# One core, a chain of two transformer blocks: the first mixer's compression with its weights as the stationary operand, and the products of its compressed attention in two lots

## The chip, the core and the metric

The kernel is one program on one core of a Trainium2 chip. Its time is device microseconds from the start to the end of an execution. All data is float32 in memory. Large matrix products are made of three products of rounded halves (float32r tiles `whi`, `wlo`, `xt`); the small ones around the change are plain float32.

## The reference

One block with a hybrid mixer (256 tokens, width 1024) is followed by a second block of two layers. Cut to the part that the change touches, in the first block's mixer:

```python
n_cmp = (S - NSA_CMP_LEN) // NSA_CMP_STRIDE + 1        # 15 blocks of 32 tokens, 16 apart
def compress(raw, pos, w1, w2):                        # raw: 2 groups of 256 tokens x 64
    blocks = raw[:, :, idx] + pos
    return jax.nn.silu(blocks.reshape(B, G, n_cmp, NSA_CMP_LEN * dh) @ w1) @ w2
k_cmp = compress(kc_raw, pos_k, w1_k, w2_k)            # w1: 2048 x 256, w2: 256 x 64
v_cmp = compress(vc_raw, pos_v, w1_v, w2_v)
...
lg = einsum(qc, k_cmp) * scale + tab_g[:, :, rel_bucket(d_cmp)]
p_cmp = masked_softmax(lg, d_cmp >= 0)                 # 8 heads x 256 tokens x 15 blocks
o_cmp = einsum(p_cmp, v_cmp)
return gc[..., 0:1] * o_cmp + gc[..., 1:2] * o_slc + gc[..., 2:3] * o_win
```

## The kernel before

Weights come in units of 128 x 2048 floats (1 MB), loaded by SyncE's queue into three buffers `raw`. For most units ScalarE makes the rounded half `whi` (four buffers, `hi_to`) and VectorE the rest `wlo` (three buffers, `lo_to`); `hi_to(k, act, u)` and `lo_to(k, dve, u)` make all units up to `u` that are not yet made. The four units 6 to 9 of the first mixer (`U_MIX + 6` to `+ 9`) hold the compression's weights `w1` (two for the keys, `s` = 0, two for the values, `s` = 1) and are read straight from `raw`. A buffer of `raw` is free for the next load when its unit has been split, or for these four when TensorE has used it.

Each engine has its own program, written out by hand; semaphores order them. The first mixer on TensorE (`mixer_tensor`) is a loop of 26 steps `i`. In each step `att.tensor` does the ordinary attention of 24 head slots in a pipeline: the scores of slot `i` (2 products), the turn of slot `i - 1` (3 transposes) and the sums of slot `i - 2` (3 products). Behind it `mixer_between_tensor` fills the step with other work, by `i`:

- steps 2 to 5: `compress_tensor(s, half)`, 8 of the 16 row pairs of a block each. `BK` (128 rows x 30 columns: 2 groups x 15 blocks) is the stationary operand, the weights of a row pair (128 x 256) the moving one, and the result, 30 x 256, gathers in bank 4 (`s` = 0) or 5 (`s` = 1).
- step 7: `compressed_tensor` turns the result, by now in `HT` behind a copy by VectorE (`compress_vector`, steps 3 and 5) and Silu by ScalarE (`compress_scalar`, step 6), into 256 x 30 by four transposes (line 1024); `compressed_vector` copies it to `HD`.
- step 8: `cmp_tensor` step 0, the products by `w2`, which wait for `HD`.
- step 12: logits of the compressed attention; steps 14 and 15: its probabilities turned into `CT` (15 rows x 2048).
- step 16: `cmp_tensor` step 5, all 16 products of `CT` with the values `VC`: 15 rows x 128 columns stationary, 15 x 64 moving, into banks 7 and 6. VectorE adds them to the output, gated, in step 16 (`cmp_vector` step 5: four operations, lines 1131 and 1134, through `add_gated`).
- steps 6 to 9, 10 to 13, 14 to 18: projections by units 10 to 15 (three products of rounded halves a piece), 12 or 24 records a step at 256 columns.

On VectorE each step holds the row maxima of slot `i` (lines 837 and 843) and, in two steps of three, the copy of slot `i - 1`'s turned probabilities (line 850), then the other work, `lo_to` of one unit in every second step from 11 to 17 among it. The sums of the third set of heads gather in banks 6 and 7 from step 18 on and so wait until the compressed attention's second half has been added (`sums_need`). Nearly all matmuls are issued by one helper, line 231, and all whole transposes by another, line 242.

A plain float32 product shows in the trace as two records (two passes); a transpose and a product of rounded halves as one.

Of the kernel before, what the change touches and what calls it, by code (L numbers as in the profile page):

```python
# [883 lines left out]
def mixer_tiles(k):  # L884
# [33 lines left out]
    k.HT = ar(k, 2560, 512, "p (s n) -> p s n", s=2)  # L918
# [78 lines left out]
def compress_tensor(k, pe, s, half):  # L997
    b, u = 4 + s, U_MIX + 6 + 2 * s + half
    w = k.raw[u % NRAW]
    pe.wait_ge(*k.s_raw[u % NRAW].after(u))  # L1000
    pe.wait_ge(*k.s_dv.after("bk", 2 * s + 1))
    for l in range(8):
        lp = half * 8 + l
        last = mm(pe, k.P[b][0:30, 0:256], k.BK[:, s, lp, :, :].rearrange("p g n -> p (g n)"),
                  w[:, l * 256:(l + 1) * 256], lp == 0, lp == 15)
    last.then_inc(*k.s_used.inc(u))


def compress_vector(k, dve, s):
    dve.wait_ge(*k.s_used.after(U_MIX + 7 + 2 * s))  # L1010
    dve.e.tensor_copy(k.HT[0:30, s, :], k.P[4 + s][0:30, 0:256]).then_inc(*k.s_ev.inc("ht", s))


def compress_scalar(k, act):
    for s in range(2):
        act.wait_ge(*k.s_ev.after("ht", s))
        act.e.activation(k.HT[0:30, s, :], k.HT[0:30, s, :], ACT.Silu).then_inc(*k.s_ea.inc("ht", s))


def compressed_tensor(k, pe, s):  # L1020
    b = 4 + s
    pe.wait_ge(*k.s_ea.after("ht", s))
    for m in range(2):
        last = pe.e.transpose(k.P[b][:, 30 * m:30 * m + 30], k.HT[0:30, s, 128 * m:128 * m + 128],
                              k.cs[0:30, C_ID:C_ID + 30])
    last.then_inc(*k.s_pe.inc("ht", s))


def compressed_vector(k, dve, s):
    dve.wait_ge(*k.s_pe.after("ht", s))  # L1030
    dve.e.tensor_copy(k.HD[:, s, :, :], k.P[4 + s][:, 0:60].rearrange("p (m n) -> p m n", m=2)).then_inc(*k.s_ev.inc("hd", s))

def cmp_tensor(k, pe, step):
    P = k.P
    if step == 0:
        for s in range(2):
            pe.wait_ge(*k.s_ev.after("hd", s))  # L1040
        pe.wait_ge(*k.s_w2.after())
        for m in range(2):
            mm(pe, P[4][:, 0:30], k.W2[:, m * 128:(m + 1) * 128], k.HD[:, 0, m, :], m == 0, m == 1)
        for g in range(2):
            for m in range(2):
                last = mm(pe, P[4][0:15, 64 + 64 * g:128 + 64 * g], k.HD[:, 1, m, g * 15:(g + 1) * 15],
                          k.W2[:, 256 + m * 64:256 + (m + 1) * 64], m == 0, m == 1)
        last.then_inc(*k.s_pe.inc("kc"))
# [21 lines left out]
    if step == 5:  # L1070
        pe.wait_ge(*k.s_ea.after("ct", 3))
        for h in range(8):
            for a in range(2):
                i = 2 * h + a
                last = mm(pe, P[7 - a][:, h * 64:(h + 1) * 64], k.CT[0:15, i * 128:(i + 1) * 128], k.VC[0:15, h // 4, :])
        last.then_inc(*k.s_pe.inc("oc"))


def cmp_vector(k, dve, step):
# [29 lines left out]
    if step == 5:  # L1109
        dve.wait_ge(*k.s_pe.after("oc"))  # L1110
# [76 lines left out]
def mixer_between_tensor(k, pe, i):  # L1187

    U = U_MIX
# [7 lines left out]
    elif i < 10:  # L1197
        if i == 7:
            for s in range(2):
                compressed_tensor(k, pe, s)  # L1200
# [11 lines left out]
    elif i < 19:  # L1212
        if i < 16:
            cmp_tensor(k, pe, i - 11)
        if i == 16:
            cmp_tensor(k, pe, 5)
# [121 lines left out]
def mixer_vector(k, dve):  # L1338
# [10 lines left out]
    for i in range(26):  # L1349
# [5 lines left out]
        if i == 3:  # L1355
            compress_vector(k, dve, 0)
        if i == 5:
            lo_to(k, dve, U + 10)
            compress_vector(k, dve, 1)
        if i == 7:  # L1360
            for s in range(2):
                compressed_vector(k, dve, s)
# [6 lines left out]
        if i in (11, 13, 15, 17):  # L1369
            lo_to(k, dve, U + 13 + (i - 11) // 2)  # L1370
# [4 lines left out]
        if i == 16:  # L1375
            cmp_vector(k, dve, 5)
# [1922 lines left out]
```

## Time and profile before

| what | value |
|---|---|
| median of 3 runs | 1649.23 us (1644.78 to 1649.86) |
| the profiled execution's own time | 1647.63 us |
| its span, first to last instruction | 1646.3 us |
| TensorE matmul busy | 1616.3 us (98%) |
| VectorE, ScalarE busy | 945.6 us (57%), 786.4 us (48%) |
| mean granted TensorE clock | 0.996 |
| the chain that ended last | TensorE 96%, VectorE 2%, ScalarE 1% |

The span and the 1.3 us around it make the execution's own time. The first mixer's steps 1 to 21 lie between 240 and 348 us of the span. A record's start in the views of time is exact to some 10 ns; its length includes the way through the array, so records in a row overlap, and the pace is read from one start to the next.

### The profile page before, as it was taken

The numbers are of one execution on the slowest core, as the hardware profiler recorded it, in microseconds if no ns is written. First come the engines' busy times: TensorE is split into PE (matmuls) and PEld (weight loads), VectorE is DVE, ScalarE is ACT, GpSimd is POOL, SyncE is SP. The second block draws the span as 40 slices with busy tenths as digits, with TensorE's granted clock in tenths as the row PEclk, the third lists the DMA queues.
The fourth block names the chain that finished last, engine by engine and source line by source line (L and its number), as shares of the span: only waits on it lengthen the run. The fifth ranks groups of instructions, "written<-read, shape, count | busy, mean of one in ns | idle before, by whom it ended". The sixth has DMA issues, their size and how long they took to land.

```text
span 1646.3 us, 29834 instructions
## 1 busy us (share of the span) xinstructions
PE 1616.3 (98%) x13094; PEld 1485.8 (90%) x13094; DVE 945.6 (57%) x1202; ACT 786.4 (48%) x1044; POOL 127.5 (8%) x117
## 2 busy tenths in 40 slices
PE   7999999999999999999998999999999999999998
PEld 7999997889999999999997889999999998899997
DVE  5544464566545655446895684546645474675545
ACT  5444444446444554445754264444544455664443
POOL 0000020000000001000376001000020001001000
PEclk9999999999999999999999999999999999999999
DMA  7744554235554465554420155554655543455551
GB/s 280 282 176 167 178 176 157 99 122 199 180 203 178 157 211 194 184 180 158 178 104 4 54 216 202 194 182 154 238 178 192 186 154 128 154 181 202 183 178 75
DMA packets 40865, 280.67 MB, mean 170 GB/s; under 512 B 4794, under 2 KB 4794, under 8 KB 8864
## 3 DMA queue, kind: packets, MB, share of 16 engines
q1 hardware_dynamic: 39024, 272.40, 46.2%
q0 software_dynamic: 1712, 6.37, 1.1%
q8 instruction: 103, 1.69, 0.4%
q14 instruction: 26, 0.21, 0.0%
HBM read 277.14 MB, written 1.08 MB: 169 GB/s over the span
## 4 chain that ended last, share of the span: by engine, by line
PE 96%; DVE 2%; ACT 1%; issue 1%; DMA 0%; SPq 0%; DVEq 0%; ACTq 0%
PE P L231 93%; PE P L242 2%; ACT whi L205 1%; DMA gb<-gains 0%; PE P L2118 0%; ACT AR L863 0%; DVE AR L371 0%; ACT xt L272 0%; DVE AR L2227 0%; DVE AR L2219 0%; DVE AR L837 0%; DVE wlo L219 0%; DVE sm L1982 0%; DVE AR L331 0%; DVE xt L279 0%
## 5 line engine op out<-in xcount | busy, mean ns | idle before, releaser
L231 PE MATMUL P<-xt,whi 128*128 128x256 f32 x5088 | 934.6, 285 | 3.0 <-ACT whi L205 1.6
L231 PEld LDWEIGHTS P<-xt,whi 128*128 128x128 f32 x5088 | 803.3, 193 | 17.8 <-issue 9.4
L231 PE MATMUL P<-xt,wlo 128*128 128x256 f32 x2544 | 702.9, 283 | 0.0
L219 DVE TENSOR_TENSOR wlo<-raw,whi 128x2048 fp32r<-128x2048 f32 x245 | 559.8, 2290 | 88.1 <-PE P L231 76.5
L205 ACT ACTIVATE whi<-raw 128x2048 fp32r<-128x2048 f32 x245 | 467.5, 1909 | 141.0 <-PE P L231 119.6
L231 PEld LDWEIGHTS P<-xt,wlo 128*128 128x128 f32 x2544 | 489.2, 192 | 0.0
L687 DVE TENSOR_TENSOR AR<-P,AR 128x256 f32<-128x256 f32 x114 | 48.4, 424 | 333.1 <-ACT AR L658 333.1
L658 ACT ACTIVATE AR<-P 128x256 f32<-128x256 f32 x114 | 43.7, 383 | 352.2 <-PE P L231 352.2
L231 PE MATMUL P<-whi,hh 128*128 128x512 f32 x504 | 197.9, 393 | 0.0
L231 PE MATMUL P<-wlo,hh 128*128 128x512 f32 x504 | 196.8, 391 | 0.0
L231 PE MATMUL P<-whi,hl 128*128 128x512 f32 x504 | 196.1, 389 | 0.0
L231 PE MATMUL P<-AR 64*64 64x64 f32 (+8 forms) x2506 | 126.9, 244 | 2.5 <-issue 1.3
L231 PE MATMUL P<-whi,xt 128*128 128x512 f32 (+2 forms) x400 | 123.8, 373 | 0.4 <-DVE xt L2529 0.4
L231 PEld LDWEIGHTS P<-AR 64*64 64x64 f32 (+6 forms) x2506 | 99.1, 144 | 18.2 <-issue 8.7
L231 PEld LDWEIGHTS P<-whi,hl 128*128 128x128 f32 x504 | 94.6, 188 | 20.0
L231 PEld LDWEIGHTS P<-whi,hh 128*128 128x128 f32 x504 | 94.9, 188 | 18.2 <-issue 0.2
L231 PEld LDWEIGHTS P<-wlo,hh 128*128 128x128 f32 x504 | 94.9, 188 | 17.5 <-issue 0.2
L690 DVE TENSOR_TENSOR hl<-AR,hh 128x256 fp32r<-128x256 f32 x126 | 55.6, 441 | 61.0 <-ACT hh L663 61.0
L231 PEld LDWEIGHTS P<-whi,xt 128*128 128x128 f32 x400 | 72.5, 189 | 13.2 <-issue 0.8
L663 ACT ACTIVATE hh<-AR 128x256 fp32r<-128x256 f32 x126 | 52.6, 418 | 63.0 <-DVE AR L687 63.0
L510 POOL TENSOR_SCALAR x<-x 128x1024 f32<-128x1024 f32 x10 | 32.5, 3261 | 577.7 <-DVE AR L687 417.3
L231 PE MATMUL P<-wlo,xt 128*128 128x512 f32 (+2 forms) x200 | 73.1, 365 | 0.0
(226 smaller groups left out, 913.0 us busy)
## 6 DMA issues: line engine op xcount, KB each, us to landing
raw<-ws SPq DMA_DIRECT2D x249, 1024.0 KB, 4.8
gb<-gains SPq DMA_DIRECT2D x14, 512.0 KB, 7.1
AR<-by_distance POOLq DMA_DIRECT2D x1, 3072.0 KB, 19.3
x<-x_in SPq DMA_DIRECT2D x2, 512.0 KB, 4.1
AR<-mem_in POOLq DMA_DIRECT2D x1, 1024.0 KB, 5.4
AR<-gains SPq DMA_DIRECT2D x2, 512.0 KB, 4.7
out<-x SPq DMA_DIRECT2D x2, 512.0 KB, 2.6
cs<-cst SPq DMA_DIRECT2D x1, 737.0 KB, 14.3
```

What stands on the lines that cost most here:

```text
L205: act.e.activation(k.whi[n % NHI][:, :], k.raw[u % NRAW][:, :], ACT.Copy).then_inc(*k.s_hi.inc(u))
L219: dve.e.tensor_tensor(k.wlo[n % NLO][:, :], k.raw[u % NRAW][:, :], k.whi[n % NHI][:, :].bitcast(F32), ALU.subtract).then_inc(*k.s_lo.inc(u))
L231: return pe.e.matmul(o, l, r, start=start, stop=stop, skip_group_check=True)
L242: return pe.e.transpose(o, i, k.cs[:, C_ID:C_ID + 128])
L510: pool.e.tensor_scalar(k.x[:, a, :], k.x[:, a, :], ALPHA / scale, None, ALU.mult).then_inc(*k.s_al.inc(t, a))
L658: act.e.activation(k.SL[:, f % 2, :], gate, ACT.Silu).then_inc(*k.s_sl.inc(t, f))
L663: act.e.activation(hh, k.HF[:, f % 2, :].rearrange("p (a t) -> p a t", a=2), ACT.Copy).then_inc(*k.s_hh.inc(t, f))
L687: dve.e.tensor_tensor(k.HF[:, f % 2, :], up, k.SL[:, f % 2, :], ALU.mult).then_inc(*k.s_hf.inc(t, f))
L690: dve.e.tensor_tensor(hl, k.HF[:, f % 2, :].rearrange("p (a t) -> p a t", a=2), hh.bitcast(F32), ALU.subtract).then_inc(*k.s_hl.inc(t, f))
```

## The change

In `compress_tensor` the operands change places: the weights of a row pair become the stationary operand in two halves of 128 columns (`m`), `BK` (128 x 30) the moving one, and the result is 128 features x 30 blocks for each half, side by side in columns 0 to 59 of the bank. This is the layout of `HD`, so the four transposes, `HT` and VectorE's four copies go, and ScalarE's Silu reads the bank and writes `HD`. The products of the compressed attention are made in two lots of four heads, in steps 16 and 17; their gated addition on VectorE moves from step 16 to 17, and `lo_to` of unit 16 from step 17 to 16.

```diff
 def compress_tensor(k, pe, s, half):
-    b, u = 4 + s, U_MIX + 6 + 2 * s + half
+    u = U_MIX + 6 + 2 * s + half
...
     for l in range(8):
         lp = half * 8 + l
-        last = mm(pe, k.P[b][0:30, 0:256], k.BK[:, s, lp, :, :].rearrange("p g n -> p (g n)"),
-                  w[:, l * 256:(l + 1) * 256], lp == 0, lp == 15)
+        for m in range(2):
+            c = l * 256 + m * 128
+            last = mm(pe, k.P[4 + s][:, 30 * m:30 * m + 30], w[:, c:c + 128],
+                      k.BK[:, s, lp, :, :].rearrange("p g n -> p (g n)"), lp + m == 0, lp == 15)
     last.then_inc(*k.s_used.inc(u))
-def compress_vector(k, dve, s):
-    dve.wait_ge(*k.s_used.after(U_MIX + 7 + 2 * s))
-    dve.e.tensor_copy(k.HT[0:30, s, :], k.P[4 + s][0:30, 0:256]).then_inc(*k.s_ev.inc("ht", s))
 def compress_scalar(k, act):
     for s in range(2):
-        act.wait_ge(*k.s_ev.after("ht", s))
-        act.e.activation(k.HT[0:30, s, :], k.HT[0:30, s, :], ACT.Silu).then_inc(*k.s_ea.inc("ht", s))
-def compressed_tensor(k, pe, s):
-    b = 4 + s
-    pe.wait_ge(*k.s_ea.after("ht", s))
-    for m in range(2):
-        last = pe.e.transpose(k.P[b][:, 30 * m:30 * m + 30], k.HT[0:30, s, 128 * m:128 * m + 128],
-                              k.cs[0:30, C_ID:C_ID + 30])
-    last.then_inc(*k.s_pe.inc("ht", s))
-def compressed_vector(k, dve, s):
-    dve.wait_ge(*k.s_pe.after("ht", s))
-    dve.e.tensor_copy(k.HD[:, s, :, :], k.P[4 + s][:, 0:60].rearrange("p (m n) -> p m n", m=2)).then_inc(*k.s_ev.inc("hd", s))
+        act.wait_ge(*k.s_used.after(U_MIX + 7 + 2 * s))
+        act.e.activation(k.HD[:, s, :, :], k.P[4 + s][:, 0:60].rearrange("p (m n) -> p m n", m=2),
+                         ACT.Silu).then_inc(*k.s_ea.inc("hd", s))
...
-    if step == 5:
+    if step in (5, 6):
         pe.wait_ge(*k.s_ea.after("ct", 3))
-        for h in range(8):
+        for h in range(4 * step - 20, 4 * step - 16):
...
-        last.then_inc(*k.s_pe.inc("oc"))
+        last.then_inc(*k.s_pe.inc("oc", step))
...
-        if i == 16:
-            cmp_tensor(k, pe, 5)
+        if i in (16, 17):
+            cmp_tensor(k, pe, i - 11)
...
-        if i in (11, 13, 15, 17):
-            lo_to(k, dve, U + 13 + (i - 11) // 2)
+        if i in (11, 13, 15):
+            lo_to(k, dve, U + 7 + (i + 1) // 2)
+        if i == 16:
+            lo_to(k, dve, U + 16)
...
-        if i == 16:
-            cmp_vector(k, dve, 5)
+        if i == 17:
+            cmp_vector(k, dve, 6)
```

TensorE in one of the steps 2 to 5, and below the @@ line in step 7 (difference of the two kernels; here one row is one product, shown by its shape out, x is how many stand in a row; `P<-raw,AR` and `P<-AR,raw` are the compression, line 1024 the transposes of `HT`):

```order
 L231 MATMUL P<-AR 128x64 x3
-L231 MATMUL P<-raw,AR 30x256 x8
+L231 MATMUL P<-AR,raw 128x30 x16
 L231 MATMUL P<-AR 128x128
 L231 MATMUL P<-AR 128x256
@@ -1194,5 +1194,4 @@
 L242 MATMUL P<-cs,AR 128x128 x3
 L231 MATMUL P<-AR 128x64 x3
-L1024 MATMUL P<-cs,AR 128x30 x4
 L231 MATMUL P<-xt,whi 128x256 x2
 L231 MATMUL P<-xt,wlo 128x256
```

Each step of the compression has 16 products in the place of 8, and step 7 loses its four transposes.

TensorE in steps 16 and 17, the same view (three of the `128x64` rows in each step are the attention's own sums, the rest the products of `CT` and `VC`):

```order
 L231 MATMUL P<-AR 128x256
 L242 MATMUL P<-cs,AR 128x128 x3
-L231 MATMUL P<-AR 128x64 x19
+L231 MATMUL P<-AR 128x64 x11
 L231 MATMUL P<-xt,whi 128x256 x2
 L231 MATMUL P<-xt,wlo 128x256
@@ -1355,5 +1354,5 @@
 L231 MATMUL P<-AR 128x256
 L242 MATMUL P<-cs,AR 128x128 x3
-L231 MATMUL P<-AR 128x64 x3
+L231 MATMUL P<-AR 128x64 x11
 L231 MATMUL P<-xt,whi 128x256 x2
```

The sixteen products of step 16 stand as eight in step 16 and eight in step 17, behind the sums of each.

VectorE from the maxima of step 16 to the split of unit 16, before (lines 837 and 843 are maxima, 850 a copy for the attention, 1131 and 1134 the gated addition out of banks 7 and 6, 219 the split):

```order
L843 TENSOR_SCALAR sm<-sm 128x2
L1131 TENSOR_TENSOR AR<-P7,sm 128x512
L1134 TENSOR_TENSOR AR<-AR 128x512
L1131 TENSOR_TENSOR AR<-P6,sm 128x512
L1134 TENSOR_TENSOR AR<-AR 128x512
L837 ISA AR,sm<-P2,AR 128x128
L837 ISA sm 128x1
L837 ISA AR,sm<-P2,AR 128x256
L837 ISA sm 128x1
L843 TENSOR_SCALAR sm<-sm 128x2
L850 COPY AR<-P3 128x384
L219 TENSOR_TENSOR wlo0<-raw1,whi1 128x2048
```

And of the change (1113 and 1116 are the lines 1131 and 1134 of before):

```order
L843 TENSOR_SCALAR sm<-sm 128x2
L219 TENSOR_TENSOR wlo0<-raw1,whi1 128x2048
L837 ISA AR,sm<-P2,AR 128x128
L837 ISA sm 128x1
L837 ISA AR,sm<-P2,AR 128x256
L837 ISA sm 128x1
L843 TENSOR_SCALAR sm<-sm 128x2
L850 COPY AR<-P3 128x384
L1113 TENSOR_TENSOR AR<-P7,sm 128x512
L1116 TENSOR_TENSOR AR<-AR 128x512
L1113 TENSOR_TENSOR AR<-P6,sm 128x512
L1116 TENSOR_TENSOR AR<-AR 128x512
```

The split of unit 16 stands ahead of step 17's maxima and copy, the gated addition behind them.

## Rows read from the trace of the kernel before

**Rows 1.** The page: span, TensorE's totals, its granted clock in 40 slices.

```profile
span 1646.3 us, 29834 instructions
...
PE 1616.3 (98%) x13094; PEld 1485.8 (90%) x13094; DVE 945.6 (57%) x1202; ACT 786.4 (48%) x1044; POOL 127.5 (8%) x117
...
PEclk9999999999999999999999999999999999999999
...
```

**Rows 2.** The waits from 240 to 345 us: total, times, longest.

```profile
...
ACT AR L863 <- DVE sm L843: 47.9, 18, 5.9
DVE AR L837 <- PE P L231: 36.5, 16, 4.7
...
```

**Rows 3.** Windows: busy time of each engine, granted clock (PEclk), DMA share.

```profile
...
321.00:324.00 3.00, 3.00 (x28) 2.93 (x27) 0.75 (x5) 1.36 (x5) 0.00 (x0) 1.00 0.60 251
324.00:327.00 3.00, 3.00 (x24) 2.93 (x23) 1.23 (x2) 0.00 (x0) 0.00 (x0) 0.88 0.00 0
...
330.00:333.00 3.00, 3.00 (x16) 3.00 (x15) 2.96 (x5) 2.44 (x5) 0.00 (x0) 0.50 0.00 0
...
```

**Rows 4.** TensorE's matmul groups, shapes apart.

```profile
...
L231 PE MATMUL P<-raw,AR 128*30 128x256 f32 x64 | 14.6, 380 | 0.0
...
L231 PE MATMUL P<-AR 15*128 15x64 f32 x32 | 3.8, 272 | 0.0
...
L231 PE MATMUL P<-AR 128*128 128x30 f32 x4 | 0.6, 267 | 0.0
...
```

**Rows 5.** TensorE in order of time, a compression step.

```profile
...
247.79 3.64 PE L231 MATMUL P<-raw,AR 128*30 128x256 f32 x16
251.36 0.92 PE L231 MATMUL P<-AR 64*128 64x128 f32 x4
...
```

**Rows 6.** TensorE, steps 6 and 7.

```profile
...
267.90 0.92 PE L231 MATMUL P<-AR 64*128 64x128 f32 x4
...
269.73 0.48 PE L231 MATMUL P<-xt,whi 128*128 128x256 f32 x2
...
272.77 0.92 PE L231 MATMUL P<-AR 64*128 64x128 f32 x4
...
275.07 0.51 PE L231 MATMUL P<-xt,whi 128*128 128x256 f32 x2
...
```

**Rows 7.** TensorE inside the products.

```profile
...
322.75 2.50 PE L231 MATMUL P<-AR 15*128 15x64 f32 x21
```

**Rows 8.** TensorE, steps 16 to 18.

```profile
...
319.98 0.92 PE L231 MATMUL P<-AR 64*128 64x128 f32 x4
...
321.21 4.49 PE L231 MATMUL P<-AR 128*128 128x64 f32 x38
325.63 0.51 PE L231 MATMUL P<-xt,whi 128*128 128x256 f32 x2
...
328.00 1.65 PE L231 MATMUL P<-AR 64*128 64x128 f32 x4
...
335.19 0.92 PE L231 MATMUL P<-AR 64*128 64x128 f32 x4
...
340.06 0.92 PE L231 MATMUL P<-AR 64*128 64x128 f32 x4
...
```

**Rows 9.** VectorE, steps 16 and 17.

```profile
...
321.61 0.17 DVE L843 TENSOR_SCALAR sm<-sm 128x2 f32<-128x2 f32 x1
325.74 0.69 DVE L1131 TENSOR_TENSOR AR<-P,sm 128x512 f32<-128x512 f32 x1 [3.96 <-PE P L231]
...
327.91 0.69 DVE L1134 TENSOR_TENSOR AR<-AR 128x512 f32<-128x512 f32 x1
...
330.99 2.28 DVE L219 TENSOR_TENSOR wlo<-raw,whi 128x2048 fp32r<-128x2048 f32 x1
...
```

**Rows 10.** TensorE ahead of the second fall of the clock.

```profile
...
803.27 2.85 PE L231 MATMUL P<-AR 12*128 12x256 f32 x12
...
```

**Rows 11.** Windows, as in rows 3, after that stretch.

```profile
...
807.60:810.90 3.30, 3.30 (x18) 3.30 (x17) 2.64 (x6) 3.30 (x7) 1.53 (x2) 0.50 0.33 134
...
```

More of the change, by code:

```diff
@@ L917, in mixer_tiles @@
     k.CT = ar(k, 13800, 2048)
-    k.HT = ar(k, 2560, 512, "p (s n) -> p s n", s=2)
     k.TM = ar(k, 2560, 512)
@@ L1039, in cmp_tensor @@
         for s in range(2):
-            pe.wait_ge(*k.s_ev.after("hd", s))
+            pe.wait_ge(*k.s_ea.after("hd", s))
         pe.wait_ge(*k.s_w2.after())
@@ L1108, in cmp_vector @@
                             k.GTv[:, :, :, 0], ALU.mult).then_inc(*k.s_dv.inc("cden", 3))
-    if step == 5:
-        dve.wait_ge(*k.s_pe.after("oc"))
+    if step == 6:
+        dve.wait_ge(*k.s_pe.after("oc", 6))
         dve.wait_ge(*k.s_dv.after("cden", 3))
@@ L1197, in mixer_between_tensor @@
     elif i < 10:
-        if i == 7:
-            for s in range(2):
-                compressed_tensor(k, pe, s)
         if i == 8:
@@ L1354, in mixer_vector @@
             dve.e.tensor_scalar(k.QB[:, 2:4, :], to_tiles(k, 5), 0.125, None, ALU.mult).then_inc(*k.s_ev.inc("qb", 1))
-        if i == 3:
-            compress_vector(k, dve, 0)
         if i == 5:
             lo_to(k, dve, U + 10)
[L1359 to L1362, printed above, removed]
         if i == 8:
```

## The prediction

> **What bounds the kernel now.** I read the page first: matmuls fill 1616.3 us of a span of 1646.3 us [rows 1], so a change is worth what it takes off TensorE's own stream, and an engine beside it matters only if TensorE comes to wait for it. The waits of the mixer's steps say who has slack: VectorE waits 36.5 us for TensorE's scores, ScalarE 47.9 us for VectorE's maxima [rows 2]; both are done early in each step and idle for the rest of it. What the other engines save (four copies on VectorE, the shorter way to Silu) is therefore worth nothing by itself. The windows then show the one odd place. The clock column goes from 1.00 to 0.88 and to 0.50 around 324 to 333 us, while TensorE is busy 3.00 of 3 us throughout and the DMA share is 0.00 [rows 3]. It is the lower of the clock's two levels, 1.2 GHz for 2.4, and it comes right behind the products of the compressed attention.
>
> **The compression.** Before, a step has 8 products, 16 records of 256 moving columns; from its first record to the next step's first score 3.57 us pass (251.36 - 247.79) [rows 5]. The change makes 16 products, 32 records, of 128 stationary columns and 30 moving ones. The trace has that shape four times, in 0.6 us together with 267 ns for one: (600 - 267) / 3 = 111 ns from start to start [rows 4]. The products of `CT`, also 128 stationary columns but 64 moving ones, run at (2.50 - 0.27) / 20 = 0.112 us a record [rows 7]. Moving columns between 30 and 64 thus don't matter, the load of 128 stationary columns sets the pace. So a lot takes 32 x 0.112 = 3.58 us, where 3.57 stood: nothing gained, nothing lost. Bounds: at best the change of shape at the entry goes (the array stays at 128 x 128 behind the sums), some 0.1 us a step, -0.4 us in all; at worst the pace is the average with entry and exit, 3.82 / 32 = 0.119 us as worked out below, which is +0.25 a step and +1.0 us in all. I take 0, since the stream is long and the steady pace is the nearest row.
>
> The Trainium skill ("TensorE: Matmul & The Clock Gate", section "LDWEIGHTS (loading the stationary operand)") has a load last its columns over 1.2 GHz, 107 ns for 128 and 25 ns for 30, whatever the rows. The trace agrees within 5 ns; by the page's figure, an estimate, a lot would be 3.42 us and the four lots 0.6 us shorter.
>
> **The transposes.** Step 7, which holds them, has 275.07 - 272.77 = 2.30 us ahead of its projection; step 6 without them 269.73 - 267.90 = 1.83 us [rows 6]. They go: -0.47 us. Silu now waits for the compression's last product (267.9) only and runs in step 6 as before; `HD` is wanted in step 8, from 279.4 on, some 5 us after ScalarE is through it. If that cover were gone, TensorE would stand at step 8 for the remainder.
>
> **The two lots.** Before, steps 16 and 17 take 335.19 - 319.98 = 15.21 us [rows 8]. What they would take at the upper clock follows from undisturbed steps. Attention alone is 1.83 us [rows 6]. Step 18 is 340.06 - 335.19 = 4.87 us [rows 8], so its 24 projection records are 4.87 - 1.83 = 3.04 us, and the 12 of step 16 half of it and the entry, 1.6 us. The 16 products put 325.63 - 319.98 - 1.83 = 3.82 us into step 16 [rows 8]; eight of them put in 3.82 - 16 x 0.112 = 2.03 us. Undivided at the upper clock: 1.83 + 3.82 + 1.6 + 1.83 + 3.04 = 12.12 us, so the fall of the clock costs 15.21 - 12.12 = 3.09 us. Divided: (1.83 + 2.03 + 1.6) + (1.83 + 2.03 + 3.04) = 12.36 us, 0.24 us for the second entry. If the division keeps the clock up: -2.85 us.
>
> Does it? Both falls inside the kernel follow a stretch in which few rows of the array work: here 32 records of 15 rows, 3.7 us with hardly a break; at 803.27 us 12 records of 12 rows over 2.8 us [rows 10], and behind them the clock stands at 0.50 [rows 11]. Lots of 1.8 us, with 1.6 us of full projection and 1.83 us of attention between them, are half as long as the first and two thirds of the second. I take that they keep the clock, without certainty.
>
> **What lies beside.** VectorE in step 17: the last product of a lot ends 325.74 - 319.98 - 1.79 = 3.97 us into the step; the four operations take 327.91 + 0.69 - 325.74 = 2.86 us [rows 9], so banks 6 and 7 are free 6.83 us into it. Step 18 begins at 6.90 us and its sums 1.23 us later (321.21 - 319.98) [rows 8]: 1.3 us of cover. Were it gone, the sums of step 18 would wait, and with them the turn of step 19. The split of unit 16 now starts at 321.61 + 0.17 = 321.78 and takes 2.28 us [rows 9]; it ends at 324.06. Step 17's maxima, queued behind it, need their scores at 325.44 + 0.95 = 326.4 us: 2.3 us of cover. The load that it frees starts 9 us earlier, into windows with a DMA share of 0.00 [rows 3].
>
> **The sum.** 0 - 0.47 - 2.85 = -3.3 us. The profiled execution's own time is 1647.63 us, its span 1646.3 and 1.3 around it; it lies 1.6 us below the median 1649.23. So 1644.3 us for a like execution, 1645.9 us against the median. Its own range is 1643 to 1648, from the bounds above.
>
> **Rivals.** A change within 0.3% (4.9 us) can't be told from none here.
>
> *The clock falls in the compression.* This one ends on the other side. In a lot of 3.58 us each record streams 30 columns in 112 ns, where 256 in some 216 ns streamed before, less than a quarter of the pace (0.27 columns a ns against 1.19). No row shows full-height records with such short streams for microseconds. Against it: the 12-row records move 256 columns each and the clock fell all the same, and the products of `CT` move more columns in the same time than the new compression does; what both stretches share is the few rows, and the compression keeps 128. Also the loads, busy 2.93 of 3 us in such a stream [rows 3], now use all 128 rows. For it: the products' 64 columns are already short, and the fall could be owed to that too. Price: each lot doubles, 3.6 us more, and attention's 1.83 us nearly, so 5 us a step. From the second step on that is three steps, 15 us, and about 3 us until the clock is back behind it, as the fall of now costs; with the gain kept, 18 - 3.3 = +14.7 us, 1664 us. A single short fall is +2 and ends near no change. It decides as soon as two steps run low.
>
> *The clock still falls between the lots.* Attention and a lot together are 3.6 us of thin work, about as long as the lot that brought the fall. Then 0.47 us is gained, 0.24 lost, and up to 3.09 us paid again: 1647 to 1649.5.
>
> *A rule of busy time.* If the clock went by TensorE's idle time alone, nothing in steps 2 to 5 or 16 and 17 would move it, and with TensorE busy 3.00 of 3 us at 0.50 [rows 3] the fall would have a cause outside of these steps: -0.47 + 0.24 = -0.2 us, 1649 us. The Trainium skill ("TensorE: Matmul & The Clock Gate", section "What's actually happening") gates the clock by how busy the engine has been, with the lower level after an idle stretch; read as busy time, the trace does not agree, since no idle time precedes the fall.
>
> *The weight loads are slower than taken.* The 111 and 112 ns are of operands in `AR`, the weights come from `raw`; at the upper bound +1.0, so -2.3 us, 1647 us. It is part of the forecast's range.
>
> **How the numbers follow.** Forecast 0.45; a fall that stays between the lots 0.20; busy time alone 0.05; a fall in the compression 0.30, of which a quarter is one short fall. The first three lie between 1643 and 1650. The range reaches to 1664 for the last and 1642.5 below: 1642.5 to 1664 leaves out what is beyond the price of three steps and a lucky low, under 0.15. Faster by over 0.3% needs 4.9 us, more than the forecast gives, though the fall of now may cost more in other executions than in the profiled one (the runs spread over 5 us): 0.14. Slower: the fall in the compression but for its short form, and a little for a wait not seen, 0.25. Within 0.3%: 0.61.
>
> **What would show it.** Right: the compression's steps still 5.5 us long each with a clock of 1.00 from 245 to 275 us; step 7 without line 1024 and 0.47 us shorter; no 0.50 between 320 and 335; steps 16 and 17 at 5.5 and 6.9 us; VectorE's gated addition over before the sums of step 18. Wrong: 0.50 in the windows from 250 on and compression steps of 10 us; a second lot at 0.22 us a record; TensorE's rows with idle time ahead of the sums of step 18.

## The result: 17 us slower, and the profile after

| | before | after |
|---|---|---|
| median of 4 runs each | 1647.80 us (1644.78 to 1649.86) | 1664.64 us (1661.26 to 1669.19) |
| ratio after / before | | 1.0105, 95% interval 1.0072 to 1.0139 |
| the profiled execution's own time | 1647.63 us | 1669.19 us |
| its span and mean granted TensorE clock | 1646.3 us, 0.996 | 1667.9 us, 0.983 |

The kernel got 16.8 us slower. The profiled execution of the changed kernel is the slowest of its four, 4.6 us above their median, so its account below shows somewhat more than the typical loss. The page of the changed kernel, against [rows 1]:

```profile
span 1667.9 us, 29949 instructions
...
PE 1634.9 (98%) x13154; PEld 1509.8 (91%) x13154; DVE 945.5 (57%) x1198; ACT 785.8 (47%) x1044; POOL 127.8 (8%) x117
...
PEclk9999995999999999999999999999999999999999
...
q8 instruction: 104, 1.70, 0.4%
```

TensorE is as full as before (98%) and busy 18.6 us longer, with 60 records more; VectorE and ScalarE are where they were. No other engine has become the limit. The clock line has a 5 in its seventh slice. Span times (1 - mean clock) gives the time lost to the lower clock: 1667.9 x 0.017 = 28.4 us, where before had 1646.3 x 0.004 = 6.6. The difference, 21.8 us, accounts for the 21.6 us by which the two spans differ (the clocks are rounded to 0.001, which is 1.6 us of a span). The windows of the changed kernel show the place (columns as in [rows 3]):

```profile
246.00:249.00 3.00, 3.00 (x31) 3.00 (x28) 1.06 (x6) 0.99 (x4) 0.00 (x0) 1.00 0.00 0
249.00:252.00 3.00, 3.00 (x23) 2.63 (x22) 0.69 (x5) 0.00 (x0) 0.00 (x0) 0.92 0.22 33
252.00:255.00 3.00, 3.00 (x16) 3.00 (x15) 0.58 (x2) 0.98 (x4) 0.00 (x0) 0.50 0.76 317
...
282.00:285.00 3.00, 3.00 (x15) 3.00 (x15) 1.35 (x6) 2.02 (x5) 0.00 (x0) 0.50 0.91 380
285.00:288.00 3.00, 3.00 (x24) 2.87 (x23) 0.00 (x0) 1.87 (x4) 0.00 (x0) 0.90 0.68 287
...
342.00:345.00 3.00, 3.00 (x17) 2.18 (x15) 1.02 (x6) 0.77 (x2) 0.00 (x0) 0.73 0.73 303
...
348.00:351.00 3.00, 3.00 (x18) 3.00 (x18) 1.76 (x3) 0.00 (x0) 0.00 (x0) 0.59 0.00 0
```

TensorE is busy 3.00 of 3 us in every one of them, and yet its clock stands at 0.50, the lower level of 1.2 GHz for 2.4, from about 251.5 to 285.6 us: the three later lots of the compression and the start of step 6. The last two rows show that it falls around the two lots of the products as well. TensorE's timeline, against [rows 5, 6] (start, length, operation, how many):

```profile
246.68 3.71 PE L231 MATMUL P<-AR,raw 128*128 128x30 f32 x32
250.32 0.92 PE L231 MATMUL P<-AR 64*128 64x128 f32 x4
...
252.78 6.98 PE L231 MATMUL P<-AR,raw 128*128 128x30 f32 x32
259.69 1.65 PE L231 MATMUL P<-AR 64*128 64x128 f32 x4
...
270.04 1.65 PE L231 MATMUL P<-AR 64*128 64x128 f32 x4
...
280.39 1.65 PE L231 MATMUL P<-AR 64*128 64x128 f32 x4
...
287.64 0.92 PE L231 MATMUL P<-AR 64*128 64x128 f32 x4
...
289.47 0.48 PE L231 MATMUL P<-xt,whi 128*128 128x256 f32 x2
...
292.51 0.92 PE L231 MATMUL P<-AR 64*128 64x128 f32 x4
```

The first lot runs at the upper clock: 250.32 - 246.68 = 3.64 us from its first record to the next score, 0.114 us a record. The second takes 259.69 - 252.78 = 6.91 us for the same 32 records. Steps 4 and 5 last 10.35 us each where 5.5 stood. Step 7 has lost its transposes: 289.47 - 287.64 = 1.83 us ahead of its projection for 2.30. Steps 16 to 19, against [rows 8]:

```profile
335.96 0.92 PE L231 MATMUL P<-AR 64*128 64x128 f32 x4
...
337.19 2.70 PE L231 MATMUL P<-AR 128*128 128x64 f32 x22
...
342.38 1.52 PE L231 MATMUL P<-AR 64*128 64x128 f32 x4
...
351.41 0.92 PE L231 MATMUL P<-AR 64*128 64x128 f32 x4
...
352.64 0.78 PE L231 MATMUL P<-AR 128*128 128x64 f32 x6
...
356.28 0.92 PE L231 MATMUL P<-AR 64*128 64x128 f32 x4
```

Step 16 takes 6.42 us and step 17 9.03; together 15.45, where the undivided lot had 15.21. One row of before that is not among those ahead of the prediction, the first score of step 8, closes the account:

```profile
278.14 0.92 PE L231 MATMUL P<-AR 64*128 64x128 f32 x4
```

| stretch of the profiled execution | before | after | difference |
|---|---|---|---|
| up to the first score of step 3 | 251.36 | 250.32 | -1.04 |
| steps 3 to 5 | 16.54 | 30.07 | +13.53 |
| step 6 | 4.87 | 7.25 | +2.38 |
| step 7 | 5.37 | 4.87 | -0.50 |
| steps 8 to 15 | 41.84 | 43.45 | +1.61 |
| steps 16 to 18 | 20.08 | 20.32 | +0.24 |
| all behind | 1306.24 | 1311.62 | +5.38 |
| span | 1646.3 | 1667.9 | +21.6 |

15.4 of the 21.6 us arise in steps 3 to 7. The rows "steps 8 to 15" and "all behind" hold falls of the clock that before's execution doesn't have at these places:

```profile
309.00:315.00 6.00, 6.00 (x51) 5.28 (x51) 3.47 (x7) 0.99 (x4) 0.00 (x0) 0.83 0.19 57
...
897.00:903.00 6.00, 4.67 (x76) 4.11 (x77) 3.17 (x8) 2.49 (x7) 2.54 (x3) 0.75 0.01 3
903.00:909.00 6.00, 4.87 (x115) 4.24 (x113) 3.00 (x7) 1.78 (x6) 3.31 (x4) 0.68 0.01 4
```

The last two windows alone cost 6 x 0.25 + 6 x 0.32 = 3.4 of the 5.38 us. Whether the change brings these two is not shown here; more on it below.

### The profile page after: what moved, and what is told of

Same layout as the page of the kernel before. It is cut to its first block, busy times and chain, and to the rows that moved or that the text cites. A ratio compares the mean times of both kernels' runs of the same rounds, so it can differ in the third digit from the quotient of the medians.

```text
span 1667.9 us, 29949 instructions
## 1 busy us (share of the span) xinstructions
PE 1634.9 (98%) x13154; PEld 1509.8 (91%) x13154; DVE 945.5 (57%) x1198; ACT 785.8 (47%) x1044; POOL 127.8 (8%) x117
## 4 chain that ended last, share of the span: by engine, by line
PE 94%; DVE 2%; ACT 2%; issue 1%; DMA 1%; POOL 0%; SPq 0%; DVEq 0%; ACTq 0%
PE P L231 91%; PE P L242 2%; ACT whi L205 1%; DMA AR<-AR 0%; DMA gb<-gains 0%; DVE wlo L219 0%; PE P L2093 0%; ACT AR L863 0%; ACT xt L272 0%; DVE AR L371 0%; DVE AR L837 0%; DVE AR L2202 0%; DVE xt L279 0%; DVE sm L1957 0%; DVE x L359 0%
## 5 line engine op out<-in xcount | busy, mean ns | idle before, releaser
L231 PEld LDWEIGHTS P<-xt,whi 128*128 128x128 f32 x5088 | 802.5, 193 | 18.6 <-issue 9.4
L231 PE MATMUL P<-AR 64*64 64x64 f32 (+7 forms) x2506 | 132.0, 249 | 3.9 <-issue 2.0
L231 PEld LDWEIGHTS P<-AR 64*64 64x64 f32 (+5 forms) x2506 | 103.3, 148 | 18.5 <-issue 8.9
```

The costliest lines, as they stand in the source:

```text
L231: return pe.e.matmul(o, l, r, start=start, stop=stop, skip_group_check=True)
```

## The experiments

Times are medians, with the lowest and highest run; a ratio is to the kernel before on the same chip in the same session, with its 95% interval. The kernel before had 1648.37, 1648.57 and 1647.74 us in the three sessions (25, 28 and 23 runs). The theory after the result: the clock falls because the new compression streams only 30 columns for each load of 128; the rivals were that the lots or the loads themselves do it. In the diffs, `...` stands for edits that are left out: the ones that carry the same change through to the other engines.

**The two lots alone.** The compression as before, the products of `CT` in steps 16 and 17.

```diff
-    if step == 5:
+    if step in (5, 6):
-        for h in range(8):
+        for h in range(4 * step - 20, 4 * step - 16):
...
-        if i == 16:
-            cmp_tensor(k, pe, 5)
+        if i in (16, 17):
+            cmp_tensor(k, pe, i - 11)
```

> The compression as before (30 columns stationary, 256 moving, transposes in step 7); only the products of the compressed attention in two lots, with the gated addition in step 17 and the split of unit 16 in step 16. Theory S (it is the short streams of the new compression that bring the clock down): no 0.50 between 245 and 290 us, and the time near the kernel before, between -3.1 us (the lots keep the clock) and +1 us (they do not). Rival L (the new order of steps 16 and 17 costs by itself, for instance by a wait of VectorE): several us slower than before, with idle time of TensorE in steps 17 and 18. Rival P (the clock falls by where an execution happens to stand, whatever the compression): a long stretch at 0.50 here too.

Measured: 1647.18 us (1646.37 to 1654.16, 10 runs), ratio 1.0008 (0.9993 to 1.0023). Its timeline of TensorE, first scores of steps 16 to 19:

```profile
321.31 0.92 PE L231 MATMUL P<-AR 64*128 64x128 f32 x4
...
327.75 1.51 PE L231 MATMUL P<-AR 64*128 64x128 f32 x4
...
336.75 0.92 PE L231 MATMUL P<-AR 64*128 64x128 f32 x4
...
341.63 0.70 PE L231 MATMUL P<-AR 64*128 64x128 f32 x3
```

The two steps take 15.44 us, as in the changed kernel. The division alone changes nothing that can be measured, and it doesn't keep the clock. In the compression the clock stays at 1.00 (24.00 us from 246 to 270), and steps 3 to 5 take 16.54 us as before.

**The compression alone.** The changed compression without transposes, the products of `CT` in one lot.

```diff
-        last = mm(pe, k.P[b][0:30, 0:256], k.BK[:, s, lp, :, :].rearrange("p g n -> p (g n)"),
-                  w[:, l * 256:(l + 1) * 256], lp == 0, lp == 15)
+        for m in range(2):
+            c = l * 256 + m * 128
+            last = mm(pe, k.P[4 + s][:, 30 * m:30 * m + 30], w[:, c:c + 128],
+                      k.BK[:, s, lp, :, :].rearrange("p g n -> p (g n)"), lp + m == 0, lp == 15)
...
```

> The new compression alone; the products in one lot in step 16 as before. Theory S: the clock at 0.50 from the first or second compression step to behind the fourth, some 34 us of it, and a time 15 to 20 us above the kernel before, that is all of the change's loss. Rival L: at most 1 us from the kernel before, since the compression's own count of records gives 32 x 0.112 = 3.58 us a step for 3.57.

Measured: 1667.95 us (1666.57 to 1670.69, 4 runs), ratio 1.0126 (1.0105 to 1.0146). The window from 246 to 270 us:

```profile
246.00:270.00 24.00, 24.00 (x116) 22.57 (x116) 2.36 (x12) 3.10 (x13) 0.00 (x0) 0.54 0.26 88
```

The whole loss is in this part: +19.6 us against +16.8 for the full change, with four runs of each; their intervals overlap, so the difference of the two is not shown. In this execution the stretch at 0.50 is longer, from about 248 to 289 us.

**The moving operand longer, 120 columns.** The changed kernel, with `BK` read four times over in each product; the added columns are copies, and nobody reads their results. The loads, their number and their data are the same.

```diff
-            last = mm(pe, k.P[4 + s][:, 30 * m:30 * m + 30], w[:, c:c + 128],
-                      k.BK[:, s, lp, :, :].rearrange("p g n -> p (g n)"), lp + m == 0, lp == 15)
+            last = mm(pe, k.P[4 + s][:, 120 * m:120 * m + 120], w[:, c:c + 128],
+                      k.BK[:, s, lp, :, :].rearrange("p g n -> p (g n)").unsqueeze(1).to_broadcast([128, 4, 30]),
+                      lp + m == 0, lp == 15)
...
```

> The changed kernel with each moving operand of the compression read four times over: 120 moving columns for 30 (three of the four copies of the result are not used; the output is the same). By the rows of before, 256 columns take 216 ns, so 120 take 101 ns and hide under the load's 112 ns: the records' pace stays. Theory S: the clock stays at 1.00 through the compression, its steps are 5.5 us again, and the time is 1 to 3.5 us under the kernel before. Rival W (a stream of full 128-column weight loads in plain float32 brings the clock down, whatever is moved): as the changed kernel, steps of 10.4 us at 0.50, +17 us. If the moving columns did set the pace, steps would be longer at a clock of 1.00.

Measured: 1651.08 us (1645.87 to 1654.55, 10 runs), ratio 1.0010 (0.9993 to 1.0026). The window from 246 to 270 us, first of the changed kernel, then of this one, and this one's timeline:

```profile
246.00:270.00 24.00, 24.00 (x131) 22.89 (x128) 3.15 (x17) 3.33 (x13) 0.00 (x0) 0.61 0.25 88
```

```profile
246.00:270.00 24.00, 24.00 (x195) 21.89 (x194) 7.99 (x31) 6.12 (x18) 0.00 (x0) 1.00 0.42 141
```

```profile
251.13 0.92 PE L231 MATMUL P<-AR 64*128 64x128 f32 x4
252.98 3.78 PE L231 MATMUL P<-AR,raw 128*128 128x120 f32 x32
256.69 0.92 PE L231 MATMUL P<-AR 64*128 64x128 f32 x4
```

Four times the columns, and the kernel is 13.6 us faster than with 30 by the medians, which are of two sessions (15.7 us by the two ratios): the clock stays at 1.00 and a step takes 5.56 us, 195 records in 24 us for 131. The gain over before that I had expected from it didn't come.

**The moving operand longer, 60 columns.** The same with two copies.

```diff
-            last = mm(pe, k.P[4 + s][:, 120 * m:120 * m + 120], w[:, c:c + 128],
-                      k.BK[:, s, lp, :, :].rearrange("p g n -> p (g n)").unsqueeze(1).to_broadcast([128, 4, 30]),
+            last = mm(pe, k.P[4 + s][:, 60 * m:60 * m + 60], w[:, c:c + 128],
+                      k.BK[:, s, lp, :, :].rearrange("p g n -> p (g n)").unsqueeze(1).to_broadcast([128, 2, 30]),
                       lp + m == 0, lp == 15)
...
```

> The same with the moving operand twice: 60 columns, nearly the 64 of the products of the compressed attention, but 128 rows for their 15. Theory S, with the number of moving columns alone in it: as few columns as in the products, behind which the clock fell, so a fall here too, perhaps a shorter one than with 30. Theory S with rows and columns both in it: rows are full, so no fall or a short one, and a time 0 to 3.5 us under the kernel before. Rival W: as the changed kernel, +17 us.

Measured: 1649.91 us (1645.15 to 1655.21, 10 runs), ratio 1.0006 (0.9991 to 1.0022).

```profile
246.00:270.00 24.00, 24.00 (x198) 22.42 (x198) 7.10 (x25) 7.59 (x23) 0.00 (x0) 1.00 0.49 170
```

```profile
249.49 0.92 PE L231 MATMUL P<-AR 64*128 64x128 f32 x4
...
255.01 0.92 PE L231 MATMUL P<-AR 64*128 64x128 f32 x4
```

With 60 columns the clock stays at 1.00 here too. The loads are busy 22.42 of 24 us; in the changed kernel they were busy 22.89. It isn't the loads. The step takes 5.52 us, what it took before. The whole kernel is as fast as before and not faster. One thing this profile shows besides: behind the lots of steps 16 and 17 the clock stands at 0.50 for 17 us, from about 322 to 339, where before had 7 us, and the two steps take 19.87 us for 15.21.

```profile
324.00:330.00 6.00, 6.00 (x26) 5.01 (x25) 1.35 (x6) 1.63 (x6) 0.00 (x0) 0.50 0.53 178
```

So what a fall at the products costs differs between executions, though TensorE's records there are the same as in the changed kernel.

**120 columns on 32 rows.** The kernel with 120 columns, its compression with rows 0 to 31 of both operands only. This leaves out three quarters of the contraction.

```diff
-            last = mm(pe, k.P[4 + s][:, 120 * m:120 * m + 120], w[:, c:c + 128],
-                      k.BK[:, s, lp, :, :].rearrange("p g n -> p (g n)").unsqueeze(1).to_broadcast([128, 4, 30]),
+            last = mm(pe, k.P[4 + s][:, 120 * m:120 * m + 120], w[0:32, c:c + 128],
+                      k.BK[0:32, s, lp, :, :].rearrange("p g n -> p (g n)").unsqueeze(1).to_broadcast([32, 4, 30]),
                       lp + m == 0, lp == 15)
...
```

> The kernel with 120 moving columns in the compression, on rows 0 to 31 of the operands alone: it leaves out three quarters of the compression's contraction. Same pace, same columns, a quarter of the rows. Theory R (rows count as well as columns): the clock falls to 0.50 in the compression as with 30 columns on 128 rows (120 x 32 = 30 x 128), steps of 10.4 us. Rival C (moving columns alone): the clock stays at 1.00 as with 120 columns on 128 rows.

Measured: 1672.32 us, one run.

```profile
246.00:270.00 24.00, 24.00 (x119) 21.65 (x119) 4.04 (x18) 3.33 (x13) 0.00 (x0) 0.60 0.25 88
```

The columns are those that kept the clock, and it falls all the same, as in the changed kernel (0.61 in this window there). So here the clock goes with the rows in use as well as with the columns streamed. This rests on one execution; but the 41 us at 0.50 in its compression are as long as with the compression alone, and no kernel that kept 128 rows and at least 60 columns there has any of it.

**The products of `CT` on 128 rows.** The kernel before, its products in one lot, with rows 15 to 127 added: those of `VC` are zeros, so the sums are what they were.

```diff
-                last = mm(pe, P[7 - a][:, h * 64:(h + 1) * 64], k.CT[0:15, i * 128:(i + 1) * 128], k.VC[0:15, h // 4, :])
+                last = mm(pe, P[7 - a][:, h * 64:(h + 1) * 64], k.CT[:, i * 128:(i + 1) * 128], k.VC[:, h // 4, :])
...
+        dve.e.memset(k.VC, 0.0).then_inc(*k.s_dv.inc("vc0"))
+        dve.wait_ge(*k.s_dv.after("vc0"))
...
-            act.e.activation(k.CT[0:15, q * 512:(q + 1) * 512], k.P[7 - q % 2][0:15, :], ACT.Copy).then_inc(*k.s_ea.inc("ct", q))
+            act.e.activation(k.CT[:, q * 512:(q + 1) * 512], k.P[7 - q % 2][:, :], ACT.Copy).then_inc(*k.s_ea.inc("ct", q))
```

> The kernel before with the products of the compressed attention on all 128 rows of the array for 15: rows 15 to 127 of VC are set to zero, those of CT are whatever the banks hold, so the output is the same. One lot, as many records, same columns (128 stationary, 64 moving). Theory R (rows in use count, as columns do): as the compression with 60 moving columns and full rows, which kept the clock, so no fall behind the products, 3 us less than before. Rival Z (zeros don't count as work): the fall stays, the time is that of before. Rival C (columns alone count, 64 are too few for 3.6 us): the fall stays too, and the two are then told apart by the compression on 32 rows.

Measured: 1643.83 us (1642.25 to 1652.34, 12 runs), ratio 0.9982 (0.9969 to 0.9996).

```profile
319.45 0.92 PE L231 MATMUL P<-AR 64*128 64x128 f32 x4
...
320.68 4.35 PE L231 MATMUL P<-AR 128*128 128x64 f32 x38
...
326.44 0.92 PE L231 MATMUL P<-AR 64*128 64x128 f32 x4
...
331.30 0.92 PE L231 MATMUL P<-AR 64*128 64x128 f32 x4
```

```profile
348.00:354.00 6.00, 5.93 (x27) 4.89 (x26) 3.75 (x10) 4.04 (x10) 0.00 (x0) 0.62 0.72 266
```

Steps 16 and 17 take 11.85 us for the 15.21 of before: the fall behind the products is gone, with all 32 records in a row and nothing changed in them but the rows, which hold zeros on one side. The second fence shows that this execution has a fall 23 us later, where before had none; so not all of the 3.4 us stayed. Whether it is the old fall moved is not shown: TensorE stood idle for 1.0 of the 9 us ahead of it.

**The lots inside the projection.** The two lots, each put in the middle of its step's projection work, away from attention's thin records.

```diff
+        if n == 0:
+            cols_piece_tensor(k, pe, U + 14, 0, 1, (4, 5))
+            cmp_tensor(k, pe, 5)
+            cols_piece_tensor(k, pe, U + 14, 0, 1, (6, 7)).then_inc(*k.s_used.inc(U + 14))
+        else:
+            cols_part_tensor(k, pe, U + 15, 1, [(0, 0)])
+            cmp_tensor(k, pe, 6)
+            cols_part_tensor(k, pe, U + 15, 1, [(0, 1)])
...
```

> Compression as before, products in two lots, but each lot in the middle of its step's projection: 6 projection records, lot, 6 in step 16; 12, lot, 12 in step 17. Theory M (the clock follows how much of the array works over some microseconds, and a lot side by side with attention is too thin): dense work now stands between attention and lot, so no 0.50 between 310 and 340 us in most executions, and 2 to 3.5 us less than the kernel before. Rival (the products themselves are enough, wherever they stand): the clock falls behind them as in the kernel with lots alone, and the time is that of before. A wait of the sums of step 18 for the gated addition is to be seen here, some 0.2 us, since the second lot ends 1.5 us later.

Measured: 1650.09 us (1644.58 to 1653.49, 12 runs), ratio 1.0010 (0.9997 to 1.0022).

```profile
294.00:300.00 6.00, 6.00 (x51) 5.06 (x50) 3.47 (x7) 0.99 (x4) 0.00 (x0) 0.83 0.14 30
...
324.00:330.00 6.00, 6.00 (x48) 5.40 (x47) 2.68 (x7) 2.42 (x9) 0.00 (x0) 1.00 0.56 193
330.00:336.00 6.00, 5.98 (x46) 5.08 (x44) 3.51 (x10) 1.53 (x1) 0.00 (x0) 1.00 0.00 0
```

In the profiled execution the clock holds through steps 16 and 17, but is lower near 298 us, behind the logits of step 12. Over its 12 runs the mean clock is 0.9941, no better than before's 0.9948. A miss: one profile with a clean stretch doesn't make a faster kernel.

**Logits with longer streams.** The kernel with products on 128 rows, and in step 12 the 15 columns of the keys read four times over (60).

```diff
-                c = (h // 2 * 2 + a) * 15
-                last = mm(pe, P[7 - h % 2][:, c:c + 15], k.QB[o:o + 64, h // 2, a * 128:(a + 1) * 128],
-                          k.KC2[o:o + 64, 15 * (h // 4):15 * (h // 4) + 15])
+                c = (h // 2 * 2 + a) * 60
+                last = mm(pe, P[7 - h % 2][:, c:c + 60], k.QB[o:o + 64, h // 2, a * 128:(a + 1) * 128],
+                          k.KC2[o:o + 64, 15 * (h // 4):15 * (h // 4) + 15].unsqueeze(1).to_broadcast([64, 4, 15]))
...
```

> The kernel with the products of the compressed attention on 128 rows, and the logits of the compressed attention in step 12 (64 rows, 15 moving columns, 32 records in some 2 us) with the 15 columns read four times over. Theory R (rows and columns in use over some microseconds count): the short falls at 295 to 301 us, seen in three profiles so far, go as well; the time is 0 to 1.5 us under that of the 128-row products alone, 3 to 6 us under the kernel before. Rival: those falls have another cause (the transposes and the attention around step 12): no change to the 128-row products alone. If 60 columns lengthened the records, step 12 would grow by up to 2 us.

Measured: 1643.86 us (1642.88 to 1647.25, 11 runs), ratio 0.9978 (0.9968 to 0.9988). As fast as without it; the mean clock went from 0.9967 to 0.9971, which these runs don't tell apart. No fall near 298 us is in its profile, but none is in that of the products on 128 rows alone either, so its worth stays open.

**Everything together.** The changed kernel with 120 columns in the compression and the lots' products on 128 rows: the change with both causes of a fall taken out.

```diff
...
-                last = mm(pe, P[7 - a][:, h * 64:(h + 1) * 64], k.CT[0:15, i * 128:(i + 1) * 128], k.VC[0:15, h // 4, :])
+                last = mm(pe, P[7 - a][:, h * 64:(h + 1) * 64], k.CT[:, i * 128:(i + 1) * 128], k.VC[:, h // 4, :])
...
```

> The changed kernel with both causes of the lower clock taken out: 120 moving columns in the compression, 128 rows in the products (still in two lots). What is left against the 128-row products alone is the change's own sum: -0.47 us for the transposes, +0.24 for the second lot, 0 to +0.2 for the lots of the compression, and under theory N (more instructions on TensorE, idle time elsewhere) +1.5 to +2.5 us. So theory N: 1 to 3 us slower than the 128-row products alone, some 1645 to 1648 us, with the idle time at 394 to 415 us. Without theory N: within 0.5 us of them.

Measured: 1646.60 us (1645.21 to 1655.71, 13 runs), ratio 0.9992 (0.9983 to 1.0000). First scores of steps 16 to 18:

```profile
320.67 0.92 PE L231 MATMUL P<-AR 64*128 64x128 f32 x4
...
325.88 0.92 PE L231 MATMUL P<-AR 64*128 64x128 f32 x4
...
332.53 0.92 PE L231 MATMUL P<-AR 64*128 64x128 f32 x4
```

The steps are clean (5.21 and 6.65 us), and still this kernel is 2.7 us slower than the two with the products on 128 rows in one lot. Its clock is as good as theirs: among runs with a mean clock of 0.998 the median is 1646.1 us here (7 runs) and 1643.6 with the products on 128 rows alone (8 runs). So some 2.5 us are owed to something other than the clock. The next kernel bears on that.

**The same number of products in the old orientation.** The kernel before, each product of the compression cut into two of 128 moving columns: 32 products more as in the change, which is 64 records (the change has 60, as it drops four transposes), and no other edit.

```diff
-        last = mm(pe, k.P[b][0:30, 0:256], k.BK[:, s, lp, :, :].rearrange("p g n -> p (g n)"),
-                  w[:, l * 256:(l + 1) * 256], lp == 0, lp == 15)
+        for m in range(2):
+            last = mm(pe, k.P[b][0:30, 128 * m:128 * m + 128], k.BK[:, s, lp, :, :].rearrange("p g n -> p (g n)"),
+                      w[:, l * 256 + m * 128:l * 256 + m * 128 + 128], lp + m == 0, lp == 15)
```

> The kernel before, with each moving operand of the compression (256 columns) cut in two of 128 columns behind the same 30-column stationary operand: as many instructions on TensorE as the changed kernel has in these steps (16 products for 8), full streams, no short ones. It separates what the changed kernel's records cost from what their number costs. Theory N (the number of TensorE's instructions costs time elsewhere: in all four kernels with the new compression TensorE stands some 0.8 us at 394 to 415 us and 1 to 2 us more between 910 and 945 us with nothing that it waits for): the same idle time here, the clock at 1.00 through the compression, and 1.5 to 2.5 us more than before. Rival F (that idle time comes from how the new compression shifts everything behind it): none at 394 to 415 us, and within 0.5 us of before apart from the short floor of each record. Pace: 128 columns at 256 / 216 ns are 108 ns, so a step stays at 5.5 us.

Measured: 1653.16 us (1648.98 to 1660.32, 11 runs), ratio 1.0037 (1.0022 to 1.0053). Its waits of TensorE, and one row of its timeline far behind the change:

```profile
PE P L231 <- issue: 2.8, 3, 1.4
```

```profile
402.04 0.47 PE L231 MATMUL P<-whi,hh 128*128 128x512 f32 x1 [0.90 <-issue]
```

The clock holds in the compression (128 columns for each load of 30), so it isn't the number of products that lowers it there. But the kernel is slower, in two parts. TensorE stands idle for 2.8 us with nothing that it waits for, where before had 1.3; the row at 402 us has its like at 414 us in the changed kernel (0.95 us) and none in before. All seven kernels with the added records have such a row between 395 and 419 us, of 0.71 to 1.14 us, and none of the five without them. And the mean clock over the runs is 0.9916 for 0.9948, with falls outside the compression; in the profiled execution the clock is at 0.50 for 14 us behind the products of step 16, where before had 7. For the second I have no cause.

All runs together. "Lost" is the mean over the runs of span x (1 - mean clock), "rest" that of span x mean clock, what the span would be at the upper clock throughout, with its standard error; "idle" is TensorE's idle time without a releaser in the profiled execution. The clock is on record to 0.001 for each run, which leaves "lost" and "rest" of a run open by 0.8 us either way, beside the standard error. The changed kernel has four runs of an earlier session, the compression alone four.

| kernel | ratio | clock | lost, us | rest, us | idle, us |
|---|---|---|---|---|---|
| before | 1 | 0.9948 to 0.9951 | 8.1 to 8.5 | 1638.6 to 1638.8 ± 0.3 | 1.3 |
| changed | 1.0105 | 0.9860 | 23.3 | 1640.4 ± 0.3 | 2.9 |
| lots alone | 1.0008 | 0.9947 | 8.7 | 1638.8 ± 0.2 | 1.2 |
| compression alone | 1.0126 | 0.9830 | 28.3 | 1638.7 ± 0.9 | 3.5 |
| 120 columns | 1.0010 | 0.9953 | 7.8 | 1641.2 ± 0.5 | 3.0 |
| 60 columns | 1.0006 | 0.9956 | 7.3 | 1640.9 ± 0.4 | 4.2 |
| old orientation in halves | 1.0037 | 0.9916 | 13.8 | 1639.5 ± 0.8 | 2.8 |
| lots inside the projection | 1.0010 | 0.9941 | 9.8 | 1638.5 ± 0.3 | 2.1 |
| products on 128 rows | 0.9982 | 0.9967 | 5.5 | 1638.4 ± 0.4 | 0.9 |
| and logits at 60 columns | 0.9978 | 0.9971 | 4.8 | 1638.5 ± 0.5 | 3.1 |
| everything together | 0.9992 | 0.9968 | 5.3 | 1640.7 ± 0.3 | 3.5 |

## Why the prediction was wrong

The forecast was 1645.9 us and the result 1664.6; what happened is the rival "The clock falls in the compression", priced at 1664.

**The step that failed** is the choice at the forecast: "what both stretches share is the few rows, and the compression keeps 128". I had two stretches with few rows and took that for the whole cause, though nothing in the trace had short columns at full height. In its place, the runs with 120, 60 and 30 columns, with the same loads and the same 128 rows, show that few columns bring the clock down too (1.00, 1.00 and 0.61 in the same window); the rows matter as well (0.60 at 120 columns on 32 rows). The forecast put this term at nothing, and in the profiled execution it cost 13.53 + 2.38 = 15.9 us. The comparison that should have weighed more stood in the prediction: 0.27 columns a ns against 1.19. It was a reason for more than 0.30. Two slips beside it: the bounds of the terms, -0.4 and +1.0 us around 1645.9, give 1645.5 to 1646.9 and not the forecast's own range of 1643 to 1648; and the full range ended at 1664, the price of this rival itself, with no room above it.

**The compression's pace** was right: forecast 3.58 us a lot at the upper clock, measured 3.64 in the first lot against 3.57 before, and with 60 columns the whole step is 5.52 us for 5.52. So weight loads from `raw` are not slower than from `AR` by anything that shows. By the figure of the Trainium skill that the prediction drew on ("TensorE: Matmul & The Clock Gate", section "LDWEIGHTS (loading the stationary operand)"), an estimate, a lot would have been 3.42 us; 3.64 was measured, and that decides. The prediction's "agrees within 5 ns" holds for 128 columns (112 ns for 107); for 30 it showed no row.

**The price of the fall** was right in size: forecast 5 us in each of three steps, measured 3.85, 4.84 and 4.84; forecast 3 us until the clock is back, measured 2.38. Over all runs, those of before from the later sessions, the clock took 23.3 - 8.5 = 14.8 us and the rest 1.6. That the rival's 14.7 us came near is partly luck: it counted 18 us for the fall, where steps 3 to 6 show 13.53 + 2.38 = 15.9, and took off 2.85 us for the lots, which gave nothing.

**The transposes** were right: 1.83 us for 2.30 ahead of step 7's projection, 0.50 us off the step for the forecast 0.47. Silu stays covered: it ends at 285.6 us in ScalarE's timeline, and step 8 begins at 292.5.

```profile
285.26 0.33 ACT L1014 ACTIVATE AR<-P 128x60 f32<-128x60 f32 x2
```

**The two lots** didn't keep the clock: 15.45 us for the forecast 12.36. Run alone they give 15.44, so the lower clock of the compression had no part in it; the rival "The clock still falls between the lots" was right for this term. This is the second step that failed: -2.85 us in the sum, nothing measured. The working at the upper clock was close. Undivided, forecast 12.12 us, measured 11.85 on 128 rows; divided, forecast 12.36, measured 5.21 + 6.65 = 11.86. The division itself costs nothing that shows, not 0.24. And what the fall cost in before's execution, forecast 3.09 us, is 15.21 - 11.85 = 3.36; with 60 columns it was more, as shown above.

**What lies beside** held, in these two steps at a partly lower clock. VectorE's last gated operation, in its timeline, begins at 349.14 us and ends at 349.83, and the sums of step 18 start at 352.6:

```profile
349.14 0.69 DVE L1116 TENSOR_TENSOR AR<-AR 128x512 f32<-128x512 f32 x1
```

**A rule of busy time** falls. The Trainium skill ("TensorE: Matmul & The Clock Gate", section "What's actually happening") gates the clock by how busy the engine has been; the trace doesn't agree with that as long as busy means time: 24.00 of 24 us at a clock of 0.61, and 24.00 of 24 at 1.00 with nothing changed but the columns of a product.

**What the prediction left out** is a cost of about 2 us that is not the clock's. Four of the kernels with some 60 records more than before have 1.6 to 2.4 us more in the column "rest" (changed, 120 and 60 columns, everything together), and 1.6 to 2.9 us more idle time without a releaser. This cost accounts for most of why the version with both causes of a fall removed gains 1 us and not the 3.8 that the transposes and a held clock add up to. What it is stays open. That it comes from the number of records is argued, not shown. For it: the idle row between 395 and 419 us stands in all seven kernels with more records and in no other, and the profile's queue of instruction transfers has 104 packets in these seven and 103 in the others. Four of the seven profiled executions also have the clock at 0.50 somewhere between 880 and 934 us, for 3 to 21 us, and none of the five others; with one execution of each kernel that is a hint and no more. Against it: the halves have only 0.9 ± 0.8 us more in "rest" and the compression alone none (1638.7 ± 0.9), and the kernel with the longer logits has 3.1 us of idle time without a releaser, with no product more, and is none the slower.

The best kernel of these is neither of the two: before, with the products of `CT` on 128 rows, 1643.83 us, or with the longer logits too, 1643.86.

## What to carry to other kernels

Swapping the operands of a small product can leave every record's pace as it was and still cost: here streams of 30 columns per load took TensorE to its lower clock although it was never idle, and everything among them ran at half speed for 34 us. Look at the granted clock in and behind each stretch of thin products (few rows, or few columns for each load), and if it falls, try to pad with copies or zeros as long as the load hides them; here 60 columns for 30 cost nothing a step and gave about 15 us back. Judge such an edit by the mean clock over many runs and not by one profile, since falls come and go at other places.

## What was not expected of the hardware

- Copied columns and rows of zeros kept TensorE's clock up: 60 columns of which 30 are copies held it at 1.00 through 24 us, and 32 records with 113 of 128 rows of the moving operand at zero had no fall behind them, with steps 16 and 17 at 11.85 us for 15.21.
- Falls of the clock differ between executions in place and length: without the one at 326 us, the kernel with 128 rows had a clock of 0.62 from 348 to 354 us, and with 60 columns in the compression the fall at the lots lasted 17 us for 7. Over the 12 runs of the kernel with 128 rows 3.0 of 8.5 us lost to the clock were gained, close to the 3.4 of the single fall.
- With some 60 records more in 13,000, in an early stretch, TensorE stands idle at a place 130 us and more behind (0.90 us at 402 us, 0.95 at 414) with no wait that the profile can name; all seven such kernels show it and none of the five others.
